# Third slab of a pair at even half groups, and slab splits regrouped around the level copies, in a two-block fp32 network on one core

## The reference, cut to what matters

```python
xbc = jax.nn.silu(causal_dwconv(xbc, conv_ssd_w) + conv_ssd_b)
y = ssd_scan(xs_h, dt, A, Bm, Cm)                 # 24 heads, 4 groups, chunks of 128
y = (y + d_skip * xs_h) * jax.nn.silu(z)          # then a norm for each group
y_sc = sc_b * causal_dwconv(sc_c * sc_x, conv_sc_w)
return jnp.concatenate([y_ssd, y_sc], axis=-1) @ w_out
```

```python
scores[t, s] = sum_k q[t, k] * k[s, k] * exp(cum[t, k] - cum[s, k])   # s <= t
o = scores @ v + (what earlier chunks left in the state)
```

## Time and profile before

| | |
|---|---|
| median of 3 runs | 1709.42 us (1709.13 to 1710.18) |
| the profiled execution's own time | 1709.01 us |
| its span, first to last instruction | 1707.2 us |
| mean granted clock of TensorE | 0.995 |
| TensorE matmuls busy | 1667.0 us, 98% of the span |
| VectorE busy | 1283.1 us, 75% |
| ScalarE busy | 1032.5 us, 60% |
| GpSimd busy | 112.0 us, 7% |
| chain that ended last | TensorE 92%, VectorE 4%, ScalarE 3%, issue 1% |
| DMA | 315.63 MB, mean 185 GB/s |

### The profile page before, as it was taken

The page is one execution under the profiler, slowest core; times in us unless marked ns, Lnnn a source line. Parts: engine busy times, 40 slices in busy tenths (PEclk is TensorE's granted clock), DMA queues, the critical chain, the costliest instruction groups (busy, mean ns, idle before and its releaser), DMA issues.

```text
span 1707.2 us, 34369 instructions
## 1 busy us (share of the span) xinstructions
PE 1667.0 (98%) x10835; PEld 1504.1 (88%) x10835; DVE 1283.1 (75%) x2361; ACT 1032.5 (60%) x1629; POOL 112.0 (7%) x101
## 2 busy tenths in 40 slices
PE   8999999999999999999999999899999999999998
PEld 7998789999999999988888888898878888878886
DVE  6866773799977777777777777789677777977776
ACT  7756554766656666654554554665466667766665
POOL 0024200343100000000000000100000000000000
PEclk9999999999999999999999999999999999999999
DMA  6542355677765555477787777543345555246553
GB/s 209 172 149 100 112 191 191 186 222 231 231 207 174 178 171 175 169 230 242 238 279 244 238 241 242 174 157 103 112 162 195 185 185 165 95 152 198 186 193 113
DMA packets 113262, 315.63 MB, mean 185 GB/s; under 512 B 12624, under 2 KB 44752, under 8 KB 112688
## 3 DMA queue, kind: packets, MB, share of 16 engines
q1 hardware_dynamic: 112352, 310.83, 55.7%
q0 software_dynamic: 848, 4.00, 0.6%
HBM read 296.43 MB, written 18.35 MB: 184 GB/s over the span
## 4 chain that ended last, share of the span: by engine, by line
PE 92%; DVE 4%; ACT 3%; issue 1%; DMA 0%; DVEq 0%; ACTq 0%; SPq 0%
PE bank L272 12%; PE bank L273 11%; PE bank L274 11%; PE bank L337 11%; PE bank L338 11%; PE bank L339 11%; PE bank L293 9%; PE bank L297 5%; PE bank L1503 3%; PE bank L1955 1%; DVE wlo L247 1%; PE bank L329 1%; PE bank L331 1%; PE bank L330 1%; PE bank L1474 0%
## 5 line engine op out<-in xcount | busy, mean ns | idle before, releaser
L247 DVE TENSOR_TENSOR wlo<-raw,whi 128x1024 fp32r<-128x1024 f32 x499 | 613.5, 1232 | 143.3 <-ACT whi L239 133.6
L239 ACT ACTIVATE whi<-raw 128x1024 fp32r<-128x1024 f32 x524 | 550.6, 1052 | 42.2 <-PE bank L331 36.0
L272 PE MATMUL bank<-x,whi 128*128 128x256 f32 (+1 forms) x1728 | 505.8, 293 | 4.6 <-DVE x L704 1.0
L274 PE MATMUL bank<-x,wlo 128*128 128x256 f32 (+1 forms) x1728 | 490.5, 284 | 0.0
L273 PE MATMUL bank<-x,whi 128*128 128x256 f32 (+1 forms) x1728 | 490.0, 284 | 0.0
L272 PEld LDWEIGHTS bank<-x,whi 128*128 128x128 f32 x1728 | 330.0, 191 | 9.0 <-issue 6.0
L273 PEld LDWEIGHTS bank<-x,whi 128*128 128x128 f32 x1728 | 330.6, 191 | 0.1
L274 PEld LDWEIGHTS bank<-x,wlo 128*128 128x128 f32 x1728 | 329.8, 191 | 0.0
L337 PE MATMUL bank<-whi,yhi 128*128 128x512 f32 x816 | 319.3, 391 | 1.8 <-DVE ylo L719 1.0
L338 PE MATMUL bank<-wlo,yhi 128*128 128x512 f32 x816 | 318.1, 390 | 0.0
L339 PE MATMUL bank<-whi,ylo 128*128 128x512 f32 x816 | 317.6, 389 | 0.0
(11 more groups left out here) (318 smaller groups left out, 1713.8 us busy)
## 6 DMA issues: line engine op xcount, KB each, us to landing
raw<-in_stream SPq DMA_DIRECT2D x524, 512.0 KB, 3.5
act_spill<-h SPq DMA_DIRECT2D x124, 128.0 KB, 3.1
h<-act_spill SPq DMA_DIRECT2D x124, 128.0 KB, 3.9
h<-in_x SPq DMA_DIRECT2D x1, 1024.0 KB, 5.1
arena<-in_keys POOLq DMA_DIRECT2D x1, 1024.0 KB, 6.0
h_spill<-h SPq DMA_DIRECT2D x1, 1024.0 KB, 7.2
arena<-h_spill POOLq DMA_DIRECT2D x1, 1024.0 KB, 6.6
arena<-in_g_final POOLq DMA_DIRECT2D x1, 512.0 KB, 8.5
```

Source lines behind the costliest of these rows:

```text
L239: nc.scalar.activation(whi[:, q * 1024:(q + 1) * 1024], raw[:, q * 1024:(q + 1) * 1024], ACT.Copy).then_inc(hi_ready, 1)
L247: nc.vector.tensor_tensor(wlo[:, q * 1024:(q + 1) * 1024], raw[:, q * 1024:(q + 1) * 1024], whi[:, q * 1024:(q + 1) * 1024].bitcast(F32), ...
L272: nc.tensor.matmul(bank[b][:, 0:T], whi[:, w], xhi[:, x], start=k == 0, stop=False)
L274: last = nc.tensor.matmul(bank[b][:, 0:T], wlo[:, w], xhi[:, x], start=False, stop=k == KT - 1)
```

## The change

In the state space part, `K_SC` moves slabs 7 to 10 of the short convolution from before half groups 7, 9, 11, 13 to before 8, 10, 12, 14. The first `y_dve` goes ahead of VectorE's part of slab 11.

In the HGRN levels, wide slab 12 goes from level 5 to behind level 6. ScalarE rounds fewer slabs ahead of each `level_exp`, according to a table of its own, and `level_exp` begins its query side when that difference is there. On VectorE `q_side(x + 1)` goes ahead of `take(x)`, the splits follow two tables, and splits 11 to 14 all stand behind the last copy.

```diff
-        K_SC = {-1: 2, 0: 3, 2: 4, 4: 5, 6: 6, 7: 7, 9: 8, 11: 9, 13: 10}
+        K_SC = {-1: 2, 0: 3, 2: 4, 4: 5, 6: 6, 8: 7, 10: 8, 12: 9, 14: 10}
@@ dve_ssd
             group_out(2 * GROUPS - 1)
+            y_dve(dve, D_WOUT, 0, 0, 4, col(Y, 0, 0, 4))
             sc_dve(dve, chain, 11)
@@ dve_wout
-            y(0)
             y(1)
@@
-        AFTER = {8: (2,), 0: (3,), 1: (4, 5), 2: (6, 7), 3: (8, 9), 4: (10,), 5: (11, 12), 6: (), 7: (13,)}
+        AFTER = {8: (2,), 0: (3,), 1: (4, 5), 2: (6, 7), 3: (8, 9), 4: (10,), 5: (11,), 6: (12,), 7: (13,)}
+        HI_AT = {8: (2,), 0: (3,), 1: (4,), 2: (5, 6), 3: (7, 8), 4: (9, 10), 5: (11,), 6: (12,), 7: (13, 14)}
+        LO_MID = {2: (5,), 3: (7,), 4: (9,)}
+        LO_AFTER = {8: (2,), 0: (3,), 1: (4,), 2: (6,), 3: (8,), 4: (), 5: (), 6: (10,), 7: (11, 12, 13, 14)}
@@ act_hgrn, level_exp
-                act.wait_ge(s("dcum"), 2 * x + 2)
+                act.wait_ge(s("dcum"), 2 * x + 1)
                 e = QK[x % 2].rearrange("p (b w) -> p b w", w=2 * m)
                 nc.scalar.activation(e[:, :, m:2 * m], e[:, :, m:2 * m], ACT.Exp).then_inc(s("e_q"), 1)
+                act.wait_ge(s("dcum"), 2 * x + 2)
                 nc.scalar.activation(e[:, :, 0:m], e[:, :, 0:m], ACT.Exp, scale=-1.0).then_inc(s("e_k"), 1)
@@ act_hgrn
-            done = 2
             for x in LEVEL_ORDER:
-                while done <= max(AFTER[x], default=0) + 1 and done < 14:
-                    slot_free(done)
-                    done += 1
+                for k in HI_AT[x]:
+                    slot_free(k)
                 if x + 2 < 8:
                     level_exp(x + 2)
-            split(14)
@@ dve_hgrn
             for x in LEVEL_ORDER:
-                if AFTER[x]:
-                    split(AFTER[x][0])
-                take(x)
                 if x < 7:
                     q_side(x + 1)
+                for k in LO_MID.get(x, ()):
+                    split(k)
+                take(x)
                 if x + 2 < 8:
                     differences(x + 2)
-                for k in AFTER[x][1:]:
+                for k in LO_AFTER[x]:
                     split(k)
-            split(14)
```

## The result

The changed kernel takes 1700.83 us, the median of 4 runs (1699.18 to 1701.72), against 1709.8 us of before beside it. The ratio is 0.9948, with a 95% interval of 0.9936 to 0.996: 8.9 us less, between 6.8 and 10.9. The prediction was 1701.7 us and a gain of 7.7. The profiled execution after takes 1701.72 us, span 1699.9.

The account below looks back on a forecast made before the run. TensorE, busy 98% of the span, was taken as the bound; 2.4 (state space) + 3.6 (levels) + 1.7 (clock) = 7.7 us off 1709.01 gives 1701.3, plus 0.41 for the median: 1701.7 us, range 1699.8 to 1705.2.

Parts of the forecast that it names:

- Term A: State space part: with slabs 7 to 10 at even half groups, half group 15 and slab 11 start 1.3 us earlier.
- Term B: Slab 11 to the first w_out product: moving the first y_dve ahead saves 1.1 us, with 1.0 us of cover.
- C: HGRN levels: late starts of levels 1, 5 and 7 go, 3.6 us, if no level waits afterwards.
- Term D: Level 7: 1.7 us gained if the clock stays up once TensorE no longer stops; bounds nothing or 1.7.
- rival 1: Slow stretch remains or turns up elsewhere: 1703.4 us, chance 0.15; opposite, one later stretch lost too: 1700.0, chance 0.06.
- Rival 4: HGRN levels: copies hand banks back late and levels wait, net 6.2 us slower, 1715.6 us; chance 0.03.

Follow-up runs that it names:

- e3: Before with only slabs 7 to 10 moved to even half groups; half group 6 to the first w_out product took 30.89 us (before 32.46).
- e7: Before with only splits 11, 12 and 13 moved behind the last copy; level 8 to wide slab 13 took 65.87 us (before 65.88).
- e8: Changed kernel with splits 10, 11 and 12 put back behind levels 4, 5 and 6; level 8 to wide slab 13 took 60.64 us.
- e9: Changed kernel with five extra VectorE products ahead of the query side of level 7; level 8 to wide slab 13 took 62.99 us.
- e11: The changed kernel itself, timed again on the same chip as the one without TensorE's eight waits; 1701.52 us, ratio to before 0.9955.
- e6: Before with only the next level's query side moved ahead of the copies; level 8 to wide slab 13 took 62.16 us (before 65.88).
- e5: Before with only wide slab 12 moved behind level 6; level 8 to wide slab 13 took 63.52 us (before 65.88).
- e4: Before with only the first y_dve moved ahead of slab 11's part; half group 6 to the first w_out product took 32.66 us.
- e2: Changed kernel with both state space edits undone, so level edits alone; 1704.77 us, ratio to before 0.9971.
- e10: Changed kernel without TensorE's eight waits for its own products behind odd half groups; 1697.04 us, ratio to before 0.9934.

## Why the prediction was right, point by point

**Term A, 1.3 us.** S without the y edit fell by 32.46 - 30.89 = 1.57 in e3. The mechanism is as stated: MM(15) was late behind slab 10's part. The size is a little low because I took 0.9 us for half group 14 and 1.39 from half group 15 to slab 11, 2.29 in all, both read from half groups that stand behind a stop or a drain; where two follow each other directly it is 188.25 - 186.36 = 1.89.

**Term B, 1.1 us.** 191.34 - 188.25 = 3.09 against 4.26: 1.17. (With the slabs already moved the edit is worth 1.3, since the wait was 1.13 there; A and B together gave 2.87 where 2.4 were forecast.) VectorE's list was close to the predicted one: the first remainder of y began 189.81 - 161.75 = 28.1 us after half group 6, where 189.1 - 160.4 = 28.7 was predicted:

```profile
189.81 0.46 DVE L719 TENSOR_TENSOR ylo<-arena,yhi 128x256 fp32r<-128x256 f32 x1
```

and ended about 1 us ahead of TensorE's need.

**Terms C and D, 3.6 and 1.7 us.** L fell by 5.24 where 5.3 were forecast, 1.7 by the clock (5.23 against 3.49 us for level 7) and 3.5 by the order. The starts were right too: `q_side(7)` ran at 1184.75, which is 51.3 us after level 8, and 1186.7 - 1135.4 = 51.3 was predicted:

```profile
1184.75 1.23 DVE L2225 TENSOR_TENSOR arena<-arena 128x1024 f32<-128x1024 f32 x1
```

**The step that was wrong** is the reason given for the largest part of C, the 2.16 us of level 7: "Before, levels 4, 5 and 6 carry splits 10, 11 and 12, 3.4 us, none of which TensorE wants before level 7 is over", and that `q_side(7)` moves because "three splits (3.4) and the copies of level 6 (2.5) stand behind it now". e7 shows that splits 11 and 12 are worth 0.0 us there, and e8 that 10 and 11 ahead of this query side cost nothing in the new order. The place of the copies and slab 12 between the levels carry it. For the 0.91 us of level 5 the reason may be right: split 10 stands in that list, and no run takes it away. The laid-out lists gave the right times because they held the wait of the copies for level 6; the sentence drawn from them compared only VectorE's load with TensorE's, and a loop through both engines is in neither sum.

**Term D** was taken as whole. It held within L in this pair of profiles, but e3 and e9 show that the slow stretch follows such a stop in 4 of 6 cases, so it is worth about 4/6 x 1.7 = 1.1 us on average, by an estimate from these six. The bounds of nothing to 1.7 us were the right thing to state. What **rival 1** calls a slow stretch elsewhere is what the first window after shows, though ahead of the change's place and by chance of the execution. It took D's 1.7 us back in the profiled pair. That the 7.3 us of the pair still lie near 7.7 is luck: S gave 0.5 us more than forecast, and 0.52 us came from the scatter between the stretches. The medians (8.9 us here, 1709.23 - 1701.52 = 7.7 us in e11) bear out the sum, but do not show D in it.

Rival 1 also put 1.7 us on one slow stretch more or less later in the program. The stop of 2.27 us of rows 9 stays in all 13 profiles, and in 8 of them the window from 1415 to 1440 us shows 0.93, which is (1 - 0.93) x 25 = 1.75 us of TensorE's time at full clock. Yet from wide slab 13 to the end it takes 505.85 to 505.94 us in the profiles without such a stretch and 506.1 to 506.5 us with it: there it costs 0.2 to 0.6 us.

The Trainium skill (TensorE: Matmul & The Clock Gate, Part 1) says that the clock gate's watching does not restart with the program and that the outcome varies from run to run. The same stop with both outcomes (1.92 us, e3 against before) agrees with the second; no run here shows the first.

**Rival 4** did not decide: in the changed kernel no level waits for a copy; in e6 level 1 does for 0.34 us and level 7 for 0.79.

The norm behind the levels kept its distance: the first sum starts 1200.26 - 1194.05 = 6.21 us after wide slab 13, 6.2 predicted, with splits 11 to 14 ahead of it:

```profile
1194.97 4.62 DVE L247 TENSOR_TENSOR wlo<-raw,whi 128x1024 fp32r<-128x1024 f32 x4
1200.26 1.28 DVE L2268 TENSOR_REDUCE arena<-arena 128x4 f32<-128x512 f32 x2 [0.67 <-ACT arena L2081]
```

## What to carry to other kernels

When an engine waits behind another that looks fully busy, do not count the other's load alone: follow the wait back, and see whether it returns to the waiting engine's own last work. If it does, work between the two ends or another order helps, and lightening the list in between does nothing while the last of these waits is for that result. Once the loop is broken, load can be the next bound, as in e5. And a removed stop on TensorE can be worth more than its length: here the clock halved behind a stop of 1.9 us in four of five profiles, for 1.7 us more.

## What the runs showed of the hardware that was not expected

The stop of 1.5 us ahead of half group 15 was followed by half clock in e4, and not in the five other profiles that have it (before, e2, e5, e6, e7). The nine repeats of before beside e10 and e11 spread over 1707.25 to 1710.29 us, as one or two slow stretches of 1.7 us would do; a part worth less is read better from stretches between two instructions than from the total. S and L agreed within 0.02 us from profile to profile at full clock, and L within 0.05 us with a slow level 7 in it.

A wait of TensorE for its own last products costs 0.25 us on average (1.96 over eight), though no other engine is late.
